# Two products of zeros on TensorE between the first scale columns and the first latent product of an encoder block

## The reference, cut to what matters

```python
mod = jnp.einsum('bd,de->be', jax.nn.silu(c), w_ada) + b_ada
sh1, sc1, gt1, sh2, sc2, gt2 = jnp.split(mod[:, None, :], 6, axis=-1)
h = _rmsnorm(x, g_mix) * (1 + sc1) + sh1
z = h @ w_in        # columns: latent q 512, latent kv 256, rope key 64, GQA q/k/v, two gates
```

## Time and profile before

| | us |
|---|---|
| median of 3 runs | 2239.27 (2237.65 to 2240.72) |
| the profiled execution | 2235.31 |
| its span in the trace | 2233.2 |
| PE busy | 2130.8 (95%) |
| DVE busy | 869.5 (39%) |
| ACT busy | 558.2 (25%) |
| mean granted TensorE clock | 0.992 of full speed |

### The profile page before, as it was taken

How to read it: one execution, slowest core, us unless ns; L and a number is a source line. 1 busy time by engine, 2 the same in 40 slices (tenths; PEclk the granted TensorE clock), 3 DMA queues, 4 the chain that set the end, 5 groups by cost and what they waited for, 6 DMA issues and landing times.

```text
span 2233.2 us, 26948 instructions
## 1 busy us (share of the span) xinstructions
PE 2130.8 (95%) x10392; PEld 1392.6 (62%) x10392; DVE 869.5 (39%) x1229; ACT 558.2 (25%) x994; POOL 4.7 (0%) x8
## 2 busy tenths in 40 slices
PE   6999999999999999999999899999999989898986
PEld 4777788888887777888888644343434344444432
DVE  4572668666666665435333400202030302021114
ACT  3254442222245564113222411010100100001002
POOL 0000000000000000000000000000000000000000
PEclk9999999999999999999999899999999999999999
DMA  8966775887771000543422699999999999999998
GB/s 321 345 227 249 268 246 177 321 312 275 281 232 28 22 9 15 194 149 118 170 85 85 245 387 421 412 421 422 422 422 422 422 421 422 422 422 422 422 418 312
DMA packets 170008, 635.63 MB, mean 285 GB/s; under 512 B 23070, under 2 KB 36556, under 8 KB 121676
## 3 DMA queue, kind: packets, MB, share of 16 engines
q1 hardware_dynamic: 165324, 626.19, 72.1%
q10 hardware_dynamic: 4608, 8.39, 1.0%
HBM read 621.94 MB, written 12.58 MB: 284 GB/s over the span
## 4 chain that ended last, share of the span: by engine, by line
PE 79%; DMA 14%; DVE 4%; issue 1%; ACT 1%; SPq 1%; DVEq 0%; ACTq 0%
PE bank L704 23%; PE bank L706 13%; DMA e_slot<-in_w_e_up 12%; PE bank L1135 12%; PE bank L1146 9%; PE bank L1099 5%; PE bank L863 4%; PE bank L754 3%; PE bank L949 2%; DMA e_slot<-in_w_e_down 1%; PE bank L1119 1%; PE bank L1041 1%; PE bank L1109 1%; PE bank L673 1%; PE bank L937 1%
## 5 line engine op out<-in xcount | busy, mean ns | idle before, releaser
L1135 PE MATMUL bank<-e_slot,xgT 128*64 128x512 f32 x2040 | 457.8, 596 | 51.2 <-DMA e_slot<-in_w_e_up 38.9
L1135 PEld LDWEIGHTS bank<-e_slot,xgT 128*64 128x64 f32 x2040 | 149.7, 137 | 332.3 <-issue 328.5
L1659 DVE TENSOR_TENSOR w_lo<-stage,w_hi 128x1024 fp32r<-128x1024 f32 (+1 forms) x168 | 202.5, 1206 | 324.1 <-ACT w_hi L1257 323.4
L1257 ACT ACTIVATE w_hi<-stage 128x1024 fp32r<-128x1024 f32 (+1 forms) x168 | 175.2, 1044 | 607.3 <-PE bank L704 340.1
L1146 PE MATMUL bank<-e_slot,heT 128*64 128x512 f32 x872 | 193.5, 595 | 0.0
L704 PE MATMUL bank<-hT_hi,w_hi 128*128 128x512 f32 x512 | 159.0, 392 | 0.0
L704 PE MATMUL bank<-hT_lo,w_hi 128*128 128x512 f32 x512 | 157.8, 389 | 0.0
L704 PE MATMUL bank<-hT_hi,w_lo 128*128 128x512 f32 x512 | 157.7, 389 | 0.0
L1727 DVE SCALAR_TENSOR_TENSOR ada_acc<-ada_tile,siluc,ada_acc 128x1024 f32<-128x1024 f32 x120 | 153.9, 1283 | 6.5 <-DMA ada_tile<-in_w_ada 1.1
L2187 DVE TENSOR_TENSOR x<-x,bank 128x512 f32<-128x512 f32 x128 | 79.6, 683 | 175.2 <-PE bank L1120 173.7
L2177 DVE SCALAR_TENSOR_TENSOR y<-bank,val,gt_row 128x512 f32<-128x512 f32 x32 | 22.0, 745 | 321.0 <-PE bank L1146 296.7
(11 more groups left out here) (326 smaller groups left out, 2758.7 us busy)
## 6 DMA issues: line engine op xcount, KB each, us to landing
e_slot<-in_w_e_up SPq DMA_DIRECT2D x128, 1024.0 KB, 21.8
e_slot<-in_w_e_gate SPq DMA_DIRECT2D x127, 1024.0 KB, 19.5
e_slot<-in_w_e_down SPq DMA_DIRECT2D x125, 1024.0 KB, 21.4
ada_tile<-in_w_ada SPq DMA_DIRECT2D x160, 512.0 KB, 5.4
stage<-in_w_in SPq DMA_DIRECT2D x96, 512.0 KB, 6.5
stage<-in_w_out SPq DMA_DIRECT2D x32, 512.0 KB, 3.6
sh_tile<-in_w_ada SPq DMA_DIRECT2D x24, 512.0 KB, 8.6
sig_gates<-sig ACTq DMA_DIRECT2D x32, 256.0 KB, 2.0
```

The lines of the kernel that those rows point to most:

```text
L1135: last = mm(bank[b0 + h][64 * e:64 * e + 64, :], xgT[:, k, e, :], e_slot[expert_slot(p, c + e)][:, j, h * W:(h + 1) * W], start=k == 0, st ...
L1257: A(w_hi[:, c % NSPLIT, :, 0:width], stage[:, c % NSTAGE, :, 0:width], ACT.Copy).then_inc(hi_ready, 1)
L1659: V.tensor_tensor(w_lo[:, c % NSPLIT, :, 0:width], stage[:, c % NSTAGE, :, 0:width], w_hi[:, c % NSPLIT, :, 0:width].bitcast(F32), ALU.sub ...
```

## The change

Two more products of the identity with `zeros` are issued on PE, after `scale_columns(0)` and before `latent_chunk(0)`. They wait for no semaphore and raise none. They write bank 6, whose content nobody reads before it is started afresh.

```diff
             for u in range(1, 4):
                 scale_unit(0, u)
             scale_columns(0)
+            for _ in range(2):
+                mm(bank[6][:, :], ident[:, :], zeros[:, :], start=True, stop=True)
             for n in range(16):
                 q, u = n // 4, n % 4
                 if n == 8:
```

## The result

The changed kernel is faster by more than was forecast. Its median was 2234.19 us (2229.45 to 2236.43, 8 runs) beside 2240.39 us for the kernel before (2237.65 to 2242.73, 8 runs): a ratio of 0.997, with a 95% interval of 0.9959 to 0.998. The profiled execution took 2229.45 us with a span of 2227.3, against 2235.31 and 2233.2. All runs together, 34 of the changed kernel and 117 of the one before, put the gain at 3.7 us in the means; how the 6.2 came about is the subject of most of what follows.

A forecast was written before the change was run, and what follows sets the result against it. PE's stream was taken as the bound nearly everywhere. Products +0, first chunk -2.4, nothing lost later: -2.4 us, the median going from 2239.27 to 2236.9 us, range 2234.6 to 2240.2.

The forecast's parts named there:

- The forecast's mechanism: In PE's opening gap, the two products keep the clock at full and cost nothing; 2.4 us gained, chance 0.42.
- The first piece: First twelve latent products of the even chunk: 5.12 us at the slow clock, 2.74 at full, so 2.38 saved.
- Rivals 1 and 3: Opening clock falls but returns sooner, gain 1.1 to 1.7 us, 0.35; slow products outlast gap, 2239.8 to 2240.2 us, 0.10.
- The weak stretch of 1.9 us: PE's 0.81 us idle plus 1.05 us of one-column work before the products; might be enough to drop the clock by itself.
- the rule of the Trainium skill: The clock gate watches how busy the engine is, so zeros count like data; the data-dependent current limiter isn't tripped by zeros.
- Rival 2: A later wait, for scale tiles or DVE's work before 155.00, takes up to all the gain; 2239.3 us, chance 0.08.
- nothing lost later: After the first chunk all of PE's work moves 2.4 us earlier, and no fixed later time takes the gain back.
- rival 4: Other clock drops change, as at 1250.74: up to 4.6 us, likelier 4, giving 2232.9 us; chance 0.05.
- within 0.2%: The whole kernel's measured time stays within about 4.5 us of no change; chance 0.93.

The follow-up runs named there:

- e_real: The changed kernel with two slices of xT (real data) in place of zeros in the two products; median 2234.34 us, ratio 0.9985 to the kernel before.
- b_look1: The kernel before, unaltered, run for a second trace; 2242.53 us.
- a_look1: The changed kernel, unaltered, run once more for its trace; 2233.19 us.
- e_again: The changed kernel, unaltered, timed again beside fresh runs of the kernel before; median 2236.36 us, ratio 0.9987.
- h_after: The changed kernel with short dense products also put into PE's later weak stretches, near 145 to 155 and 1249 to 1260 us; median 2234.69 us, ratio 0.9983.

## Why the prediction was right and wrong

**What was right.** The forecast's mechanism happened in every one of the five traces of the changed kernel: the clock stays at full level, the products hide in the gap, and the latent products start when DVE lets them. The products at full clock took 1.96 us (1.88 was taken). The first piece gained 5.12 - 2.94 = 2.18 us by the profiled pair, where 2.38 was worked out; the difference is that the first and the last of the six pairs took 0.56 and 0.54 us from start to start and not 0.457. Rivals 1 and 3 did not occur; zeros kept the clock just as data did (1.00 from 30 to 44 us in `e_real` and in the kernel after). The weak stretch of 1.9 us ahead of the products was not enough for a drop. Of the rule of the Trainium skill that was weighed ("TensorE: Matmul & The Clock Gate", Part 1) the traces agree with the part on the gate, which watches how busy the engine is.

**Rival 2** seems to come true in part in the profiled pair. Of the 2.78 us by which PE was ahead at the second quarter's scale, 0.77 were gone by the fourth columns: PE now idled 0.40 us there, waiting for `sc_rows`, where before it did not wait.

```profile
104.28 1.05 PE L729 MATMUL bank<-ones,sc_rows 128*128 128x1 f32 x8 [0.40 <-DVE sc_rows L1738]
```

But the kernel before has that wait too, in `b_look1`, and the changed kernel lacks it in `a_look1` and `e_again`, where from the second quarter's scale to the fourth columns it took 66.97 and 67.73 us, against 67.62 after and 66.85 before. So the wait is not shown to come from the edit.

```profile
109.22 1.05 PE L729 MATMUL bank<-ones,sc_rows 128*128 128x1 f32 x8 [0.37 <-DVE sc_rows L1736]
```

**What was wrong is what the later drops of the clock do: the sum has them at nothing ("nothing lost later"), and "How the numbers follow" leaves rival 4 out of the range.** Between the two profiled executions the edit gave 2.18 us, and later drops that fell elsewhere gave 2.0 and 3.7 more, of which 1.1 and 1.5 us were lost again on the way. I saw that a drop at 1250 could come or go with 4 us, called it a spread rather than a shift, and then gave it 0.05 and left it out of the range. Its size was about right, 3.7 us, although the drop was 17.1 us long and not 9.2. The runs show that it isn't rare: near 1250 us 12.0 or 8.4 us, behind it 15.6 or 13.6, near 155 us 31.3 or 29.4, between 85 and 130 us drops of 3.4 us that came or didn't. In the traces these stretches differ by 3.7, 1.9, 3.2 (from the shift columns near 120 us to the correction) and 1.9 us (between the third and the fourth columns). Together that is 10.7 of the 12.7 us between the fastest and the slowest of 117 runs of the kernel before.

For the scatter I had taken half of the 3.1 us between three runs. The first comparison of eight runs against eight then lay 2.5 us (3.1 in the means) beyond the gain that all runs together give: none of the first eight runs of before was under 2237 us, while of all 117 more than a fifth are under 2235. The forecast of 2.4 us itself, as the worth of the edit, lies just under the 2.6 to 4.8 that all the runs give, and inside the 2.0 to 4.5 of the runs without the first comparison. The term for the first piece was taken from one trace; in `b_look1` the same drop costs 2.8. With 2.2 to 2.8 for it, the rest, about 1 us, is either scatter or the moved place, and the runs don't settle which. That the forecast fits the traces so well is the mechanism; that the first result lay so far from it is chance as far as the runs show.

The chances followed the same error: 0.93 for "within 0.2%" (4.5 us) would be fair for the gain of 3.7, whose interval reaches just beyond, but not for a comparison of eight runs.

## What to carry to other kernels

A gap of 2.7 us on TensorE behind a stretch of one-column products cost this kernel 2.2 to 2.8 us, through half-clock work behind the gap, not through the gap. One or two dense dummy products in it, which end before the awaited data are there, took that away at no cost; look for such gaps by the granted clock behind them, and check that the products end inside the gap. Before forecasting a few microseconds, list all the drops of the clock in the trace and ask which of them could fall elsewhere in another execution: most of the scatter of the runs comes from them, and three runs don't show it.

## What the runs showed of the hardware

- The clock's drop in the opening was there in all traces without products in the gap, for 6.8 us each time, and in none with them. A single product (two matmuls, 1.11 us) was enough in the one trace of it, with 1.7 us idle behind it.
- In one program the later drops differ from execution to execution in place and length. After the same idle of 1.76 us near 1247 the clock stayed up for 6.9 us in one trace of the changed kernel (until 1253.40), and in another (`a_look1`) it fell 0.7 us behind it and was at half through the same products (8.4 and 12.0 us). Nor does it take an idle engine: in `h_after` PE was busy without a gap from 1250 on, with transposes and the router's 16-column products, and the clock fell at 1252.9, 4.6 us behind nine dense products. Later in that trace it was still full after 3.42 us of idle, at 1268.67, and fell at 1270.0.

```profile
1252.00:1253.00 1.00, 1.00 (x12) 0.96 1.10 467
1253.00:1254.00 1.00, 1.00 (x7) 0.50 1.03 434
```

- A drop costs only where PE is the bound: at 144 us it cost 0.4 us and gave them back, since PE then waited less for DVE, at 155 us the same length cost 1.6.
